# Second-phase transposes moved from TensorE to DMA, with five output buffers, paired score steps and a row-wise conv-state store

## The chip, the cores and the metric

One Trainium2 chip, all 8 NeuronCores, the same program on each core with its own data (one prompt sequence of 8192 tokens, and 16 of the 128 sample sequences with 8 tokens each). No core talks to another. The metric is the device time in microseconds (us) of the slowest core. The engines are TensorE (PE), VectorE (DVE), ScalarE (ACT), GpSimd (POOL) and SyncE (SP); SP and ACT issue DMAs on hardware queues (q1 and q10 in the profile), POOL on a software queue (q0).

## The reference

One layer of a hybrid decoder, cut to what matters:

```
xn = rmsnorm(x, g_attn);  q,k,v,B,C,h = split(xn @ w_in)          # 3072 columns
for g, (window, d) in enumerate([(128,1),(512,4),(2048,16)]):     # 4 heads of 64 per group
    s = q_g . k_g[t - d*(0..128)] / 8;  o_g = softmax(s) @ v_g;  lse_g = logsumexp(s)
attn = concat(o_g * softmax_over_groups(lse)_g)                    # 768 columns
u = C * h;  y = conv3(past ++ u);  conv = B * y                    # 256 columns
x1 = x + concat(attn, conv) @ w_out
x2 = x1 + relu(rmsnorm(x1, g_mlp) @ w_up)**2 @ w_down
out = rmsnorm(x2, g_fin)
```

It runs over the prompt (keys of the same sequence) and over the samples (keys from three caches of 128, 512 and 2048 rows, then the 8 new ones). Outputs besides `out`: the last rows of K and V of each group, and the last two rows of u (the conv state) for prompt and samples. For the samples the K/V outputs are the caches shifted by 8 rows, which the kernel copies DRAM to DRAM.

## The kernel before

All matmuls are bf16 with f32 accumulation. There are two phases with one order of work written out in Python; each engine walks the same list of steps and does its part, and semaphores tie them.

**First phase** (`make_plan`, `tensor_a`, `scalar_a`, `vector_a`, `sync_a`). Four super-tiles of 2048 tokens. For each: a block of 24 conv tiles (B, C, h projections), then for each of the three groups a block of 24 projection tiles (V, then Q and K). A tile is 8 or 16 matmuls into one of two PSUM banks and one evacuation by ACT or DVE; it is called a slot. While the tiles of one block run, the 16 attention chunks (128 queries) of the block before are spread between them: scores (step `S`: 8 matmuls, then one exponential on ACT), mask (`M`, DVE, one slot later), PV (PE, two slots later) and `O` (three slots later: DVE copies the 128 x 260 result from PSUM to one of two SBUF buffers `osb`, line 1029, and SP stores it to the DRAM tensor NZ, line 1316). The samples' projections come in one block after super-tile 0: their K and V rows go to `kvss` and from there to DRAM by 48 small stores on SP. The samples' conv state is loaded and stored by POOL with four DMAs each way (lines 1258 and 1253), 4 bytes at a time since channels lie on partitions: `in_=ubs[cc][:, :, 8 + j]` to `convs[:, j, ...].rearrange("b p -> p b")`. POOL also casts weights to bf16 DRAM to DRAM (`precast`, line 1248), computes the first tap of the convolution (line 1272), and at the end loads w_up and w_down.

**Second phase** (`tensor_b`, `scalar_b`, `vector_b`, `sync_b`). 33 tiles T, each of 256 tokens (the last, the samples', of 128) in subtiles of 128. The list `SLOTS` says what is done after each of the 36 slots c of tile T besides the MLP's own work, which is `up` c (8 matmuls, line 739) and `down` c-4 (4 matmuls, line 750): mostly the preparation of tile T+1.

- `LN`, `LX`, `LC`, `ST`: loads of NZ, x and conv output, store of y (SP)
- `a`: DVE normalises the attention sums into `attn_n` (which shares its memory with `xn1`)
- `b`: PE transposes `attn_n` (6 transposes, line 663), ACT copies PSUM to `attnT` (line 890)
- `c`: the output projection, two halves (line 678), DVE adds x (1126), ACT computes the norm (875 to 879)
- `n`: DVE scales to `xn1` (1133); `d`: PE transposes it (8 transposes, line 688), DVE multiplies by the gain into `xn1T` (1141)
- `sT`, `sS`, `sP`: one of 52 batches of the samples' cached attention: PE transposes the cached keys `sK` (8 transposes, line 701), DVE copies them (1091); scores; PV

Tile 0 is prepared in the last 16 slots of the first phase (`FIRST_B`), where only attention chunks are left. POOL starts w_up's load when the last projection is done and most of w_down's when the last NZ store has landed (lines 1278 to 1285). At slot 13 of every even tile ACT issues one sample's three cache copies (line 906; 4080, 1008 and 240 KB).

Of the kernel before, what the change touches and what calls it, by code (L numbers as in the profile page):

```python
# [44 lines left out]
class Waits:  # L45
# [6 lines left out]
    def wait_ge(self, sem, v):  # L52
        if v > self.got.get(sem.name, 0):
# [7 lines left out]
           (2, "b", 0, 0), (2, "LN", 1, 0), (3, "a", 0, 1), (4, "c", 0, 0, 0), (5, "b", 0, 1), (5, "LN", 1, 1),  # L61
           (6, "c", 0, 0, 1), (8, "c", 0, 1, 0), (9, "n", 0, 0), (10, "c", 0, 1, 1), (11, "d", 0, 0), (13, "n", 0, 1),
           (14, "d", 0, 1)]
# [48 lines left out]
def make_plan():  # L112
# [25 lines left out]
    def block(tiles, chunks, xs):  # L138
# [3 lines left out]
        for i, a in enumerate(chunks):  # L142
            at.setdefault(i * (ns - 1) // len(chunks), []).append(a)
        for i, tile in enumerate(tiles):
# [6 lines left out]
            if P.slot == 40:  # L151
                P.add("ldsc")
            if P.slot == 160:
                P.add("stcs")
# [37 lines left out]
    for st in range(4):  # L192
# [10 lines left out]
        for g in range(3):  # L203
# [41 lines left out]
            if st == 0 and g == 2:  # L245

                tiles = [(kind, None, dict(g=gg, t=t, p=p, copies=2 - t, xb=17)) for gg in range(3)
                         for kind, t, p in (("sq", 0, 0), ("sq", 0, 1), ("sq", 1, 0), ("sq", 1, 1))]
# [7 lines left out]
                          new("nS", 2, "act", 1), conv("C", 1), conv("H", 1), new("nP", 2, None, 2), new("nZ", 2, "dve", 2)]  # L256
# [3 lines left out]
                P.smp.update({(kw["kind"], kw["cc"]): kw for kind, kw in P.steps if kind == "proj" and kw["kind"] == "sconvH"})  # L260
# [29 lines left out]
def build_nc():  # L290
# [52 lines left out]
    ybuf = [mem.alloc("ybuf%d" % i, [128, 512], F32) for i in range(2)]  # L343
# [7 lines left out]
    osb = [mem.alloc("osb%d" % i, [128, 4, 65], F32) for i in range(2)]  # L351
# [7 lines left out]
    mem.off += 768  # L359
# [66 lines left out]
    B_M, B_T = 6, 7  # L426
# [14 lines left out]
    with ExitStack() as es:  # L441
# [15 lines left out]
        s_stnz = [sem("st_nz%d" % i) for i in range(2)]  # L457
# [7 lines left out]
        s_nm, s_stkvs, s_stcs = sem("n_masked"), sem("st_kvs"), sem("st_cs")  # L465
        s_ldk, s_ldv = sem("ld_cache_k"), [sem("ld_cache_v%d" % i) for i in range(2)]
        s_kt, s_ktc, s_ss, s_se, s_sm, s_sp, s_so = (sem("s_kt"), sem("s_kt_sb"), sem("s_scores"), sem("s_exp"),
                                                    sem("s_masked"), sem("s_pv"), sem("s_sum"))
# [297 lines left out]
        def copy_out(e, W, eng, a):  # L766
# [4 lines left out]
            if what in ("qk", "v", "kvt"):  # L771
# [4 lines left out]
                if a["kb"] == 2:  # L776
                    W.wait_ge(s_stkvs, 48 * 16)
# [681 lines left out]
```

## Time and profile before

| | |
|---|---|
| time, median of 3 runs | 3246.47 us (3242.42 to 3248.24) |
| time of the profiled execution | 3248.41 us |
| its span, slowest core (3) | 3246.7 us |
| spans of the 8 cores | 3194.0 to 3246.7 us, mean granted TensorE clock 0.979 to 0.987 |
| PE busy | 3035.3 us, 93% of the span |
| DVE, ACT, POOL busy | 41%, 33%, 6% |
| first phase, to the last projection of core 3 | about 1014 us |
| one second-phase tile with samples' batches | 66.7 us |
| one second-phase tile without them (from tile 27 on) | 65.2 us |

The profile is of one execution on the slowest core. "Idle before" tells for how long an engine had nothing to run before an instruction, and who released it. In the chain of waits the span is followed back from the last instruction, so only what stands there can shorten it. A DMA's "us to landing" runs from its issue to its last byte.

### The profile page before, as it was taken

How to read it: one execution, taken by the hardware profiler on the slowest of the kernel's cores; microseconds unless marked ns; L12 is line 12 of the kernel's file. 1: busy time of each engine (PE TensorE's matmuls, PEld its weight loads, DVE VectorE, ACT ScalarE, POOL GpSimd, SP SyncE). 2: the span in 40 equal slices, each digit the busy share in tenths (PEclk: the TensorE clock that was granted, in tenths of full speed). 3: DMA queues.
4: the chain of work that ended last, by engine and by line, in shares of the span. 5: the costliest groups of instructions: out<-in, count | busy, mean ns of one | idle time of the engine just before them, and what ended most of it. 6: DMA issues, size and time to landing. Idle time of an engine off the chain costs nothing.

```text
span 3246.7 us, 65561 instructions; the slowest of 8 cores (3194.0 to 3246.7 us)
## 1 busy us (share of the span) xinstructions
PE 3035.3 (93%) x23299; PEld 1948.8 (60%) x23299; DVE 1334.1 (41%) x2927; ACT 1080.6 (33%) x2399; POOL 187.3 (6%) x232
## 2 busy tenths in 40 slices
PE   5997859899997799999999999999999999999998
PEld 2654435565554466666666666666666666666665
DVE  5355426637444234333343333333343333433332
ACT  4244225436334223222232323323232233323232
POOL 3101200101000000000000000000000000000000
PEclk9998979999998899999999999999999999999999
DMA  9124925536134825444254343543535425333130
GB/s 198 37 67 115 79 43 130 129 70 149 34 131 178 206 51 132 104 103 120 55 141 109 86 119 58 155 109 69 122 64 145 121 57 125 77 117 107 38 114 21
DMA packets 168411, 331.62 MB, mean 102 GB/s; under 512 B 31840, under 2 KB 124000, under 8 KB 165984
## 3 DMA queue, kind: packets, MB, share of 16 engines
q1 hardware_dynamic: 94080, 172.92, 16.5%
q0 software_dynamic: 70672, 67.19, 15.9%
q10 hardware_dynamic: 3344, 87.30, 9.2%
q8 instruction: 198, 3.24, 0.5%
q14 instruction: 117, 0.96, 0.1%
HBM read 309.57 MB, written 176.39 MB: 150 GB/s over the span
## 4 chain that ended last, share of the span: by engine, by line
PE 84%; DMA 4%; ACT 3%; issue 3%; DVE 3%; SPq 1%; another core or an unknown queue 1%; POOL 0%; ACTq 0%; DVEq 0%; POOLq 0%
PE pp L750 28%; PE pp L739 26%; PE pp L566 12%; PE pp L678 7%; PE pp L533 4%; DMA NZ<-osb 3%; ACT junkB L875 1%; PE pp L536 1%; PE pp L688 1%; DMA w_in_sb<-w_in 1%; PE pp L582 1%; SPq L1328 1%; PE pp L701 1%; PE pp L663 1%; PE pp L511 1%
## 5 line engine op out<-in xcount | busy, mean ns | idle before, releaser
L739 PE MATMUL pp<-xn1T,w_up_sb 128*128 128x256 bf16 (+1 forms) x8448 | 1071.2, 271 | 29.3 <-ACT hr L901 26.6
L750 PE MATMUL pp<-w_down_sb,h1T 128*128 128x512 bf16 x4160 | 1057.9, 379 | 17.9 <-DMA w_down_sb<-w_down_b 17.9
L739 PEld LDWEIGHTS pp<-xn1T,w_up_sb 128*128 128x128 bf16 x8448 | 804.1, 98 | 281.1 <-issue 39.3
L901 ACT ACTIVATE hr<-pp 128x256 bf16<-128x256 f32 (+1 forms) x1056 | 394.6, 380 | 1181.6 <-PE pp L739 1173.9
L1150 DVE TENSOR_TENSOR h1T<-hr 128x256 bf16<-128x256 bf16 (+1 forms) x1056 | 301.0, 289 | 1003.1 <-ACT hr L901 936.5
L750 PEld LDWEIGHTS pp<-w_down_sb,h1T 128*128 128x128 bf16 x4160 | 402.7, 98 | 299.6 <-issue 19.0
L566 PE MATMUL pp<-xnT,w_in_sb 128*128 128x512 bf16 x2304 | 536.6, 382 | 24.2 <-DMA w_in_sb<-w_in 8.8
L566 PEld LDWEIGHTS pp<-xnT,w_in_sb 128*128 128x128 bf16 x2304 | 212.0, 98 | 268.9 <-issue 37.2
L678 PE MATMUL pp<-w_out_sb,attnT 128*128 128x512 bf16 x1040 | 249.7, 384 | 9.0 <-DMA attnT<-cvT 9.0
L858 ACT ACTIVATE PT<-pp 128x1024 bf16<-128x1024 f32 x171 | 174.2, 1023 | 145.3 <-PE pp L586 143.8
L1022 DVE TENSOR_TENSOR PT<-PT,mask 128x1024 bf16<-128x1024 bf16 (+1 forms) x192 | 129.4, 674 | 198.8 <-ACT PT L858 185.3
L875 ACT ACTIVATE junkB<-xtB 128x1024 bf16<-128x1024 f32 x130 | 137.1, 1055 | 195.4 <-DVE xtB L1126 192.0
L678 PEld LDWEIGHTS pp<-w_out_sb,attnT 128*128 128x128 bf16 x1040 | 102.3, 99 | 133.7 <-issue 13.9
L1126 DVE TENSOR_TENSOR xtB<-xtB,pp 128x512 f32<-128x512 f32 x130 | 89.5, 688 | 218.1 <-PE pp L678 218.0
L533 PE MATMUL pp<-w_in_sb,xnT 128*128 128x256 bf16 x1368 | 165.8, 278 | 8.6 <-issue 5.2
L533 PEld LDWEIGHTS pp<-w_in_sb,xnT 128*128 128x128 bf16 x1368 | 142.3, 118 | 23.0 <-issue 10.4
L1295 POOL DMA_DIRECT2D sK<-ck x52 | 38.7, 744 | 1668.4 <-PE pp L701 1668.4
L1158 DVE TENSOR_TENSOR xtB<-xtB,pp 128x512 f32<-128x512 f32 x130 | 80.7, 682 | 81.1 <-PE pp L750 81.1
L602 PE MATMUL pp<-V,PT 128*128 128x65 bf16 x624 | 60.4, 196 | 45.1 <-DVE PT L1022 26.4
L1029 DVE COPY osb<-pp 128x260 f32<-128x260 f32 x192 | 79.9, 421 | 48.5 <-DMA NZ<-osb 47.4
L1141 DVE TENSOR_TENSOR xn1T<-pp,g_mlp_sb 128x1024 bf16<-128x1024 bf16 x65 | 79.6, 1225 | 28.2 <-PE pp L688 28.0
L936 DVE TENSOR_TENSOR xnT<-pp,g_attn_sb 128x1024 bf16<-128x1024 bf16 x64 | 78.3, 1223 | 29.3 <-PE pp L511 28.7
(136 smaller groups left out, 1984.0 us busy)
## 6 DMA issues: line engine op xcount, KB each, us to landing
kvs<-ck ACTq DMA_DIRECT2D x16, 4080.0 KB, 21.2
xt<-xp SPq DMA_DIRECT2D x64, 512.0 KB, 5.3
xtB<-xp SPq DMA_DIRECT2D x64, 512.0 KB, 3.8
yp<-xtB SPq DMA_DIRECT2D x64, 512.0 KB, 3.1
NZ<-osb SPq DMA_DIRECT2D x192, 130.0 KB, 2.3
NZt<-NZ SPq DMA_DIRECT2D x64, 390.0 KB, 4.6
kvs<-ck ACTq DMA_DIRECT2D x16, 1008.0 KB, 6.4
sK<-ck POOLq DMA_DIRECT2D x52, 256.0 KB, 6.7
```

What stands on the lines that cost most here:

```text
L533: ins = e.matmul(b[:, i * 256:(i + 1) * 256], lhsT=toks, rhs=wi[:, kc, 512:768], start=kc == 0, stop=kc == 7)
L566: ins = e.matmul(b[:, 0:128] if smp else b, lhsT=wi[:, kc, col:col + 128], rhs=xr, start=kc == 0, stop=kc == 7)
L678: ins = e.matmul(bank(b_bank(T)[1]), lhsT=attnT[q % 2][:, kc, :], rhs=w_out_sb[:, kc, half[0] * 512:(half[0] + 1) * 512], start=kc == 0, s ...
L739: ins = e.matmul(bank(v % 2)[:, 0:N], lhsT=w_up_sb[:, i // 8, kc, (i % 8) * 128:(i % 8 + 1) * 128], rhs=xn1T[T % 2][:, kc, 0:N], start=kc ...
L750: ins = e.matmul(psD[s][:, half * 512:(half + 1) * 512], lhsT=h1T[v % NH][:, s * 128:(s + 1) * 128], rhs=w_down_sb[:, i, half * 512:(half ...
L858: e.activation(out=PT[k % NPT][:].rearrange("p b q x -> p (b q x)"), in_=ps.rearrange("p b x -> p (b x)"), func=AF.Exp, scale=0.125).then_ ...
L875: e.activation(out=junk, in_=src, func=AF.Square, accum_out=accs[0][r]).then_inc(s_bn, 1)
L901: e.activation(out=hr[v % NHR][:, 0:N], in_=bank(v % 2)[:, 0:N], func=AF.Relu).then_inc(s_hr, 1)
L1022: e.tensor_tensor(out=pt, in0=pt, in1=mask, op=ALU.mult).then_inc(s_mask, 1)
L1126: e.tensor_tensor(out=xh, in0=xh, in1=bank(b_bank(T)[1]), op=ALU.add).then_inc(s_x1, 1)
L1150: e.tensor_tensor(out=h1T[v % NH][:, 0:N], in0=hr[v % NHR][:, 0:N], in1=hr[v % NHR][:, 0:N], op=ALU.mult).then_inc(s_h1, 1)
L1158: e.tensor_tensor(out=xh, in0=xh, in1=psD[s][:, half * 512:(half + 1) * 512], op=ALU.add).then_inc(s_x2, 1)
```

## The change

Six edits:

1. **Transposes by DMA.** In the second phase the steps `b`, `t` (new, after `n`) and `sT` are DMA transposes issued by SP, SBUF to SBUF, 2-byte elements. PE's 44 transposes per tile and their PSUM copies go; `d` is now only the multiplication by the gain, in place in `xn1T`. The slots move: `b` right behind `a` (slots 5 and 9), `c` in slots 13 to 19 in place of 15 to 21, `t` in 20 and 24, `d` in 26 and 30, `sT` in 13 and 25.
2. **Five `osb` buffers** in place of two. For their room the conv buffer `ybuf` becomes the same memory as `Csb`.
3. **Samples' conv state by rows.** A new tile `su` computes C and h for the samples with tokens on partitions (8 matmuls of 512 columns), ACT and DVE form the product in `kvss`, and POOL stores two 1 KB rows per sample, 16 DMAs. The old store of four DMAs goes. The load (`ldsc`) is the same 4-byte pattern, cut in 16 pieces, one every second slot.
4. **Scores of two chunks behind one another**: chunks come in pairs in one slot, the second one's mask a slot later; both PV steps then stand behind one another.
5. POOL's loads of w_in for groups 1 and 2 come later (x tiles 13 and 16 in place of 7 and 12).
6. `FIRST_B` has the slots for tile 0's transposes.

```diff
 class Plan / make_plan
-            at.setdefault(i * (ns - 1) // len(chunks), []).append(a)
+            at.setdefault(i // 2 * 2 * (ns - 1) // len(chunks), []).append(a)
...
-            for a in at.get(i, ()):
+            for j, a in enumerate(at.get(i, ())):
                 P.add("S", **a)
-                P.later(1, "M", **a)
+                P.later(1 + j, "M", **a)
                 P.later(2, "PV", **a)
...
-    osb = [mem.alloc("osb%d" % i, [128, 4, 65], F32) for i in range(2)]
+    NO = 5
+    osb = [mem.alloc("osb%d" % i, [128, 4, 65], F32) for i in range(NO)]
...
 SLOTS (excerpt)
-                 7: [("y", -1, 1), ("ST", -1, 1), ("LX", 1, 1), ("b", 1, 0)], 9: [("a", 1, 1)], 11: [("b", 1, 1), ("LN", 2, 0)],
+                 7: [("y", -1, 1), ("ST", -1, 1), ("LX", 1, 1)], 9: [("a", 1, 1), ("b", 1, 1)], 11: [("LN", 2, 0)],
...
 tensor_b
-                    for kc in range(6):
-                        ins = e.transpose(out=pst[:, kc, :], in_=attn_n[:, kc * 128:(kc + 1) * 128], identity=ident[:])
-                    ins.then_inc(s_aT, 1)
...
 vector_a, step O
-                    if k >= 2:
-                        W.wait_ge(s_stnz[k % 2], 16 * (k // 2))
+                    if k >= NO:
+                        W.wait_ge(s_stnz[k % NO], 16 * (k // NO))
...
 pool
-                elif kind == "stcs":
-                    W.wait_ge(s_free["dve"], P.smp["sconvH", 1]["first"])
-                    for cc in range(2):
-                        for j in range(2):
-                            e.dma_start(out=convs[:, j, cc * 128:(cc + 1) * 128].rearrange("b p -> p b"),
-                                        in_=ubs[cc][:, :, 8 + j], allow_slow_non_contiguous=True).then_inc(s_stcs, 16)
+                elif kind == "proj" and a["kind"] == "su":
+                    W.wait_ge(s_free["dve"], a["first"])
+                    for bb in range(NSB):
+                        e.dma_start(out=convs[bb, :, :], in_=kvss[bb * 8 + 6:bb * 8 + 8, 256:512]).then_inc(s_stcs, 16)
...
 sync_b
+                elif kind == "b":
+                    q = nsubs_before(T) + i
+                    W.wait_ge(s_an, q + 1)
+                    if q >= 2:
+                        W.wait_ge(s_m, 2 * (q - 1))
+                    e.dma_start_transpose(out=attnT[q % 2][:, 0:6, :], in_=attn_n).then_inc(s_aT[q % 2], 16)
+                elif kind == "t":
...
+                    e.dma_start_transpose(out=xn1T[sl][:, :, i * 128:(i + 1) * 128], in_=xn1[:]).then_inc(s_xT1[q % 2], 16)
+                elif kind == "sT":
...
+                    e.dma_start_transpose(out=sKTc[:].rearrange("p u k t -> p (u k) t"),
+                                          in_=sK[:].rearrange("p u c -> p (u c)")).then_inc(s_kt, 16)
```

TensorE's order in the middle of a second-phase tile, before (L739 is `up`, L750 `down`, L678 the output projection `c`, L701 the transposes of cached keys, L663 those of `attn_n`):

```order
L739 MATMUL pp<-xn1T_9_120,w_up_sb_112 128x256 x8
L750 MATMUL pp<-w_down_sb_141,h1T_20_131 128x512 x4
L663 MATMUL pp<-ident_43,xn_8_119 128x128 x6
L739 MATMUL pp<-xn1T_9_120,w_up_sb_112 128x256 x8
L750 MATMUL pp<-w_down_sb_141,h1T_15_126 128x512 x4
L739 MATMUL pp<-xn1T_9_120,w_up_sb_112 128x256 x8
L750 MATMUL pp<-w_down_sb_141,h1T_16_127 128x512 x4
L739 MATMUL pp<-xn1T_9_120,w_up_sb_112 128x256 x8
L750 MATMUL pp<-w_down_sb_141,h1T_17_128 128x512 x4
L739 MATMUL pp<-xn1T_9_120,w_up_sb_112 128x256 x8
L750 MATMUL pp<-w_down_sb_141,h1T_18_129 128x512 x4
L678 MATMUL pp<-w_out_sb_111,attnT_6_117 128x512 x8
```

The same place after the change (there `up` is L714, `down` L725, `c` L675):

```order
L714 MATMUL pp<-xn1T_10_122,w_up_sb_113 128x256 x8
L725 MATMUL pp<-w_down_sb_142,h1T_19_131 128x512 x4
L714 MATMUL pp<-xn1T_10_122,w_up_sb_113 128x256 x8
L725 MATMUL pp<-w_down_sb_142,h1T_20_132 128x512 x4
L675 MATMUL pp<-w_out_sb_112,attnT_6_118 128x512 x8
L714 MATMUL pp<-xn1T_10_122,w_up_sb_113 128x256 x8
L725 MATMUL pp<-w_down_sb_142,h1T_15_127 128x512 x4
L714 MATMUL pp<-xn1T_10_122,w_up_sb_113 128x256 x8
L725 MATMUL pp<-w_down_sb_142,h1T_16_128 128x512 x4
L675 MATMUL pp<-w_out_sb_112,attnT_6_118 128x512 x8
```

The transposes between the MLP's matmuls are gone, and the output projection follows the fourteenth `up` of the tile in place of the sixteenth.

SP's order for one second-phase tile before, from the conv loads of the next tile on (L1377 `LC`, L1384 `ST`, L1371 `LX`, L1365 `LN`):

```order
L1377 DMA attnT_6_117<-cvT 128x2x128
L1377 DMA attnT_7_118<-cvT 128x2x128
L1384 DMA yp<-xtB_3_114 128x1024
L1371 DMA xtB_3_114<-xp 128x1024
L1384 DMA yp<-xtB_3_114 128x1024
L1371 DMA xtB_3_114<-xp 128x1024
L1365 DMA NZt_4_115<-NZ 128x780
L1365 DMA NZt_5_116<-NZ 128x780
```

And after (L1350 `LC`, L1376 `ST`, L1344 `LX`, L1338 `LN`, L1358 `b`, L1364 `t`, L1370 `sT`):

```order
L1376 DMA yp<-xtB_3_115 128x1024
L1344 DMA xtB_3_115<-xp 128x1024
L1358 DMA_TRANSPOSE attnT_6_118<-xn_8_120 128x6x128
L1376 DMA yp<-xtB_3_115 128x1024
L1344 DMA xtB_3_115<-xp 128x1024
L1358 DMA_TRANSPOSE attnT_7_119<-xn_8_120 128x6x128
L1338 DMA NZt_4_116<-NZ 128x780
L1338 DMA NZt_5_117<-NZ 128x780
L1370 DMA_TRANSPOSE sKTc_139<-sK_136 128x8x128
L1364 DMA_TRANSPOSE xn1T_10_122<-xn_8_120 128x8x128 x2
L1370 DMA_TRANSPOSE sKTc_139<-sK_136 128x8x128
L1350 DMA attnT_6_118<-cvT 128x2x128
```

Six transposes are now in SP's queue; each of the two `b` stands directly behind a load of x.

In the first phase TensorE ran one chunk's scores and PV between two projection tiles (L582 and L586 are scores, L602 and L603 PV, L566 a projection tile):

```order
L582 MATMUL pp<-Q_33_76,K_35_78 128x128 x2
L586 MATMUL pp<-Q_33_76,K_35_78 128x128 x2
L582 MATMUL pp<-Q_33_76,K_35_78 128x128 x2
L586 MATMUL pp<-Q_33_76,K_35_78 128x128 x2
L566 MATMUL pp<-xnT_52,w_in_sb_8_51 128x512 x8
L582 MATMUL pp<-Q_33_76,K_35_78 128x128 x2
L586 MATMUL pp<-Q_33_76,K_35_78 128x128 x2
L582 MATMUL pp<-Q_33_76,K_35_78 128x128 x2
L586 MATMUL pp<-Q_33_76,K_35_78 128x128 x2
L566 MATMUL pp<-xnT_52,w_in_sb_8_51 128x512 x8
L602 MATMUL pp<-V_37_80,PT_38_81 128x65
L603 MATMUL pp<-V_37_80,PT_38_81 128x65
```

After the change (L583, L587 scores, L603, L604 PV, L567 projection) two chunks' scores stand together, and so do two chunks' PV:

```order
L567 MATMUL pp<-xnT_52,w_in_sb_8_51 128x512 x8
L583 MATMUL pp<-Q_31_74,K_33_76 128x128 x2
L587 MATMUL pp<-Q_31_74,K_33_76 128x128 x2
L583 MATMUL pp<-Q_31_74,K_33_76 128x128 x2
L587 MATMUL pp<-Q_31_74,K_33_76 128x128 x2
L583 MATMUL pp<-Q_31_74,K_33_76 128x128 x2
L587 MATMUL pp<-Q_31_74,K_33_76 128x128 x2
L583 MATMUL pp<-Q_31_74,K_33_76 128x128 x2
L587 MATMUL pp<-Q_31_74,K_33_76 128x128 x2
L567 MATMUL pp<-xnT_52,w_in_sb_8_51 128x512 x16
L603 MATMUL pp<-V_35_78,PT_37_80 128x65
```

Fewer changes between scores and projection tiles are left, and two tiles in a row have none beside them.

## Rows read from the trace of the kernel before

**Rows 1.** Span and granted clock of core 7.

```profile
core 7: 3245.1 us, clock 0.981
```

**Rows 2.** Core 3: length; PE, PEld, DVE, ACT, POOL busy; clock; DMA share; GB/s.

```profile
399.84:498.50 98.66, 59.63 (x514) 36.22 (x513) 23.90 (x43) 23.20 (x28) 1.95 (x4) 0.78 0.38 48
665.04:717.60 52.56, 52.56 (x515) 33.75 (x513) 23.82 (x43) 23.20 (x28) 1.95 (x4) 1.00 0.36 77
1485.78:1552.50 66.72, 65.97 (x496) 43.92 (x494) 25.14 (x64) 20.17 (x52) 2.96 (x4) 1.00 0.57 145
```

**Rows 3.** Costliest groups: the transposes (count; busy us, mean ns; idle before).

```profile
L688 PE MATMUL pp<-ident,xn 128*128 128x128 bf16 x520 | 40.0, 220 | 0.3 <-DVE xn L1133 0.3
...
L663 PE MATMUL pp<-ident,xn 128*128 128x128 bf16 x384 | 32.5, 222 | 0.0
...
L701 PE MATMUL pp<-ident,sK 128*128 128x128 bf16 x416 | 31.7, 219 | 0.0
```

**Rows 4.** Timeline of PE in one tile: start us, us, instructions.

```profile
1497.36 0.50 PE L663 MATMUL pp<-ident,xn 128*128 128x128 bf16 x6
1497.69 1.04 PE L739 MATMUL pp<-xn1T,w_up_sb 128*128 128x256 bf16 x8
...
1499.43 1.04 PE L739 MATMUL pp<-xn1T,w_up_sb 128*128 128x256 bf16 x8
```

**Rows 5.** Timelines of SP and of DVE in one tile.

```profile
1498.06 0.35 SPq L1371 DMA_DIRECT2D xtB<-xp  x1
...
1501.38 0.16 DVE L1077 TENSOR_TENSOR stats<-NZt 128x4 f32<-128x4 f32 x1
...
1519.09 11.22 SPq L1377 DMA_DIRECT2D attnT<-cvT  x2
...
1528.19 0.75 DVE L1133 TENSOR_SCALAR xn<-xtB,stats 128x1024 bf16<-128x1024 f32 x1
...
1538.78 0.74 DVE L1133 TENSOR_SCALAR xn<-xtB,stats 128x1024 bf16<-128x1024 f32 x1
```

**Rows 6.** DMA issues: queue, count, KB each, median us to landing.

```profile
kvs<-ck ACTq DMA_DIRECT2D x16, 4080.0 KB, 21.2
...
xtB<-xp SPq DMA_DIRECT2D x64, 512.0 KB, 3.8
...
NZ<-osb SPq DMA_DIRECT2D x192, 130.0 KB, 2.3
...
convs<-ubs POOLq DMA_DIRECT2D x4, 8.0 KB, 51.6
```

**Rows 7.** The same for DMAs issued from 1513 to 1520 us.

```profile
attnT<-cvT SPq DMA_DIRECT2D x1, 64.0 KB, 12.4
```

**Rows 8.** Chain of waits, core 3: start us, us, what.

```profile
417.59 41.94 DMA NZ<-osb
...
951.61 13.95 DMA NZ<-osb
...
1020.40 16.85 DMA NZ<-osb
...
1067.13 13.98 DMA w_down_sb<-w_down_b
...
1102.56 17.25 another core or an unknown queue
```

**Rows 9.** Timeline of POOL: the conv-state store's issue.

```profile
371.06 4.65 POOL L1253 DMA_DIRECT2D convs<-ubs  x4 [0.25 <-issue]
```

**Rows 10.** Chain of waits, core 7.

```profile
410.91 13.77 issue
...
437.00 19.04 DMA NZ<-osb
```

**Rows 11.** Chain of waits, core 3, around scores and PV.

```profile
465.90 1.83 PE pp L566 x8
...
467.98 1.73 PE pp L566 x8
```

More of the change, by code:

```diff
@@ L342, in build_nc @@
     Csb = [mem.alloc("Csb%d" % i, [128, 512], F32) for i in range(2)]
-    ybuf = [mem.alloc("ybuf%d" % i, [128, 512], F32) for i in range(2)]
+    ybuf = Csb
     cvo = [mem.alloc("cvo%d" % i, [128, 512], BF16) for i in range(2)]
@@ L456, in build_nc @@
         s_hk, s_hv = sem("halo_k"), sem("halo_v")
-        s_stnz = [sem("st_nz%d" % i) for i in range(2)]
+        s_stnz = [sem("st_nz%d" % i) for i in range(NO)]
         s_cvch, s_cv, s_cvtail, s_tap = sem("conv_chain"), sem("conv_out"), sem("conv_tail"), sem("conv_tap")
@@ L519, in tensor_a @@
                     W.wait_ge(s_xnT, a["xb"])
[L520 to L521 removed]
+                    wi = w_in_sb[0] if what[-1] in "BCHu" else w_in_sb[1 + a["g"]]
+                    if what[-1] in "BCHu":
                         W.wait_ge(s_ldw[0], 16)
@@ L882, in scalar_b @@
             for kind, T, i, *half in events:
[L883 removed]
                 n = NORM.get((kind, T, i))
[L885 to L891 removed]
+                if kind == "c" and half[0] == 1:
                     q = nsubs_before(T) + i
@@ L959, in vector_a @@
                         continue
+                    if what == "su":
+                        W.wait_ge(s_proj, a["full"])
+                        W.wait_ge(s_uc, 1)
+                        e.tensor_tensor(out=kvss[:, 256:512], in0=bank(n % 2)[:, 256:512], in1=kvss[:, 0:256],
+                                        op=ALU.mult).then_inc(s_free["dve"], 1)
+                        continue
                     if what[-1] != "H":
@@ L1039, in vector_a, with stored @@
                                   ).then_inc(s_hk, 1)
+        def stored(W, n):
+            for i in range(NO):
+                W.wait_ge(s_stnz[i], 16 * ((n + NO - 1 - i) // NO))
         def phase_a_left(W):
@@ L1236, in pool @@
             for kind, a in STEPS:
-                if kind == "xc" and a["k"] in (7, 12):
-                    load_w_in(1 if a["k"] == 7 else 2)
+                if kind == "xc" and a["k"] in (13, 16):
+                    load_w_in(1 if a["k"] == 13 else 2)
                 elif kind == "xc" and a["k"] == 8:
@@ L1282, in pool @@
                     W.wait_ge(s_pv, 192)
-                    for i in range(2):
-                        W.wait_ge(s_stnz[i], 16 * 96)
+                    stored(W, 192)
                 e.dma_start(out=w_down_sb[:, lo:hi, :], in_=w_down_v[:, lo:hi, :]).then_inc(s_wd[k], 16)
@@ L1352, in sync_b @@
                     W.wait_ge(s_xT, 65)
-                    for k in range(2):
-                        W.wait_ge(s_stnz[k], 16 * 80)
+                    stored(W, 160)
                 elif kind in ("LN", "LC"):
                     phase_a_left(W)
-                    for k in range(2):
-                        W.wait_ge(s_stnz[k], 16 * (88 if T < 2 else 96))
+                    stored(W, 176 if T < 2 else 192)
                 if kind == "up" and T == 0 and i == 0:
```

147 lines of the change are left out of this document (56 added, 91 removed), and 10 rows, old and new, of tables (FIRST_B, SLOTS).

## The prediction

> **What bounds the kernel now.** I read the stretches first. A second-phase tile takes 66.7 us and PE is busy for 66.0 of them, at the full granted clock; DVE has 25 us of work in it, ACT 20 (third of [rows 2]). That phase is some 2130 of the 3247 us, so there the time is PE's own work and what leaves PE leaves the span, as long as nothing else comes late. The costliest groups then give what could leave: 520, 384 and 416 transposes [rows 3]. In the first phase two equal blocks of 24 projection tiles and 16 chunks take 98.7 and 52.6 us (first two of [rows 2]): the same 59.6 against 52.6 us of PE work, but 39 us of idle PE and a mean clock of 0.78 in the first. The chain of waits names the idle time: 41.9 us of NZ<-osb from 417.6 on, then 14.0 and 16.9 us at the end of the phase, and 14.0 and 17.3 us behind w_down [rows 8].
>
> **Transposes off PE.** Six transposes occupy PE from 1497.36 to 1497.69, until the next `up` begins: 0.33 us, 55 ns each [rows 4] (the mean of 220 ns in [rows 3] is latency in a pipeline). Tile 0's two subtiles lie in the transition and don't count. What counts is (384/6 - 2) x 0.33 = 20.5 us, (520/8 - 2) x 8 x 0.055 = 27.7 us and 416 x 0.055 = 22.9 us: 71 us. DVE loses its copy of the keys and ACT its copy of attnT, which were hidden.
>
> What must hide the new transfers: a slot is 1.74 us (1497.69 to 1499.43) [rows 4]. Where the trace has no SBUF-to-SBUF transpose, I bound its landing by the nearest rows: 2.3 us (130 KB NZ store) and 3.8 us (512 KB load) below, 12.4 us above, for 64 KB issued on SP's queue while the 4080 KB cache copy was in flight [rows 6, 7]. A transpose moves 192 or 256 KB, so I take 4 us from issue, plus the rest of what stands ahead of it on the queue.
>
> - `b` of subtile 0 is issued behind the x load of 1498.06. DVE starts `a` of subtile 1 at 1501.38 [rows 5] and now waits there for the transpose, since `attn_n` is one buffer: 3.0 us after the issue at 1498.4. Behind the waiting instruction stand the h1T squares, which `down` needs four slots after `up`: 7 us, less the 2 us of ACT and DVE in between. So landing within 3 + 5 = 8 us costs nothing. The x load ahead lands at 1498.06 + 3.8 = 1501.9; with 4 us more it is 1505.9, that is 7.5 us after the issue. Hidden, but by half a microsecond: this is the tightest place, 32 times.
> - `t` of subtile 0 follows `n`. The two `n` write at 1528.19 and 1538.78 [rows 5], four slots and one half of `c` apart as in the new order; less the 0.75 us write and 0.44 us of transposes that is 9.4 us for the landing, plus DVE's 5. In every even tile the cache copies run: they are issued at slot 13, near 1485.8 + 13 x 1.74 = 1508.4, and the largest lands 21.2 us later [rows 6], about 1530; `t` is issued at 1528.2 - 2 slots - 1.1 us of transposes + 0.75 = 1524.4, and even if it lands only 4 us behind the copies that is 1534, where the second `n` would start (1533.8). Hidden.
> - `t` of subtile 1 has six slots, 10.4 us. `sT` is issued at the time the copies start and scored 10 slots later, 24 us with the four halves of `c`: hidden too.
> - SP issues six more DMAs per tile and stands still for each condition. Behind `sT` (waits for the key load) are `t` and the next tile's stores; the key load was landed long before in the trace. The row at 1519.09 shows SP waiting 11.2 us inside a pair of loads without anybody waiting for it [rows 5].
>
> So nothing is taken off the 71 us; the ends are 71 and, with 12.4 us for each `b`, 71 - 32 x 4.4 = -70 us.
>
> **Conv state by rows.** POOL issues the store at 371.06 [rows 9]; its landing takes 51.6 us for 8 KB [rows 6], and until 460 the NZ stores are stuck. The block that this hits costs 98.66 - 52.56 = 46.1 us too much [rows 2]. On core 7 the same place shows 13.8 + 19.0 = 32.8 us [rows 10]. 16 DMAs of 2 KB in 1 KB rows are no such load: -46 on core 3, -33 on core 7 (ends 0 and -50). Against it: one tile of 8 matmuls of 512 columns, 1.7 us like the projection tile in [rows 11], and 16 DMAs on POOL at 1.2 us for each instruction at most (4.65/4) [rows 9], up to 19 us in which the next block's first tap is late. The tap's wait reaches PE only through the next copy of the same channels, six tiles (10 us) later, which hides most: +3 (0 to +12). The load cut in 16 pieces lies in a block where it moved nothing before: 0.
>
> **Pairs of chunks.** A projection tile behind scores takes 1.83 us, behind PV 1.73 [rows 11]. 88 pairs save one such change each: 9 us. ACT gets two exponentials in a row, but its work in such a block is 23.2 of 52.6 us (second of [rows 2]), and it stays the same: fits. In the three conv blocks DVE is the fuller engine and bursts could cost what pairs give: -9 (ends -18 and +10).
>
> **Five buffers.** With three more buffers PE and DVE run three chunks on (6 us) before a late store stops them. Of the 14.0 us at 951.6 [rows 8] I take off 8. At the phase's end the stores share the queues with w_up's load; of 16.9 us and the smaller waits behind it perhaps 20 go, w_down's load starts as much earlier since it waits for the last store, but the 31 us behind w_down (14.0 + 17.3) remain, and tile 0's four transposes now go through busy DMA queues, 12.4 us each in place of about 2 on PE and ACT. Net -10 (ends -35 and +25). The later w_in loads: 0.
>
> **The sum** on core 3's execution of 3248.4 us: -71 - 46 + 3 - 9 - 8 - 10 = -141, 3107. On core 7, 3245.1 [rows 1] + 1.7 us around the span - 71 - 33 + 3 - 9 - 8 - 10 = 3119. The slowest core decides, and part of what core 7 lost was at a low clock: 3113. The runs shown have their median 1.9 us under the profiled one: **3111 us**.
>
> **A rule that speaks against it.** The Trainium skill, "VectorE: DVE Perf Modes", section "The three transpose paths", gives 390 ns for a 128x128 bf16 transpose on TensorE and 1309 ns through DMA. This trace has 55 ns of PE time for the first, since such transposes overlap; the second no run shows yet. As an estimate from that page, eight in series would be 10.5 us and six 7.9 us, and `b` would land at 1501.9 + 7.9 = 1509.8, 11.4 us after its issue: 3.4 us late in each of 32 tiles, 109 us. "DMA: Bandwidth & Descriptors", "Latency and other measured facts", has 261 GB/s for transposes, by which 256 KB would be about 1 us plus the fixed cost, as an estimate.
>
> **Rivals.**
> 1. *The transposes land a little late.* Between 8 and 12.4 us after issue: every microsecond over 8 is 32 us in all. For it: the half microsecond of margin at `b`. Against: the 2.3 and 3.8 us of plain DMAs. Middle 10.2 us: 3111 + 70 = 3181 us.
> 2. *The stall at 400 us stays.* POOL's weight casts are in the same software queue, and they rather than the 4-byte store could hold up NZ. For it: the casts stand in that queue too. Against: 8 KB that needs 51.6 us. 3111 + 46 = 3157 us.
> 3. *Slower: a serial transpose.* If a DMA transpose takes more than 12.4 us, its price per tile at `b` is its landing less 8, from 14.4 us on also at the first `t` and soon at the second, each on the way to the next tile's first `up`. At 16 us: 8.0 + 1.6 + 0.7 = 10.3 us x 32 = 330 us, 3441 us. It is slower than before from a loss of 4.2 us per tile, a landing of 12.2 us. For it: small elements are what the store of 4-byte pieces suffers from (8 KB in 51.6 us), and a transpose has 2-byte elements. Against: nothing else in the trace.
>
> **Chances.** Forecast 0.64, rival 1 0.14, rival 2 0.09, rival 3 0.13. The forecast's own range is 3075 to 3150. The range of 8 in 10 goes from 3070 (the good ends of pairs and buffers, 9 + 25 us less, and some us for core 7's clock) to 3225, which takes in rival 2 and most of rival 1 and leaves rival 3 out. 0.2% (6 us) is about what a measurement can tell; between the cases almost nothing lies there: faster 0.86, same 0.02, slower 0.12.
>
> **What would show it.** Second-phase tiles of 64.2 us with samples' batches (66.7 - 4 x 0.44 - 2 x 0.33 = 64.3); transposes landing in 4 to 8 us; no wait of DVE on attn_n that reaches PE; no idle PE around 400 to 460 us; the two block lengths equal at some 52 us. Wrong if: DVE's `a` waits over 5 us for the transpose and PE's `up` or `down` waits for h1T or xn1T, or the last chunks' waits grow because tile 0's transposes stand behind the weight loads.

## The result and the profile after

The changed kernel takes 3520.2 us (median of four executions; 3479.8 to 3586.5) against 3246.6 us of before: 1.080 times as long, 95% interval 1.071 to 1.090. The forecast was 3111 us. Executions in which the cores of one die ran at a lower granted clock (here one, without which the median is 3511.1 us) are left out of every ratio and of every time from here on. The runs below were made on three chips, on which the kernel before took 3243 to 3248 us, so a difference of a few us between two of them means nothing.

The page is that of core 6, the slowest of the profiled execution (3511.1 us). Its chain is 67% PE and 13% DMA. Two of its DMA queues, SP's and ACT's (packets, MB, share of 16 engines):

```profile
q1 hardware_dynamic: 268832, 216.20, 31.5%
...
q10 hardware_dynamic: 3344, 87.30, 10.3%
```

Where PE waited (engine, line, releaser: us in total, times, longest):

```profile
PE pp L689 <- DMA sKTc<-sK: 141.5, 9, 37.5
PE pp L675 <- DMA attnT<-xn: 134.7, 7, 40.3
PE pp L603 <- DVE PT L1000: 50.3, 31, 8.5
PE pp L714 <- issue: 38.4, 2, 25.2
```

The first and second are the sample scores and the output projection, both waiting for a transpose: 276 us in only 16 waits. So the typical transpose is not slow; a few are very slow. Core 6 is not special in this: on the other seven the two waits come to 115 to 261 us. The DMA issues say the same. First the view of the issues (count, KB, median landing) with the counterparts of [rows 6], then the three transposes by tile (issue time min/median/max in ns; landing min/median/max in us).

```profile
kvs<-ck ACTq DMA_DIRECT2D x16, 4080.0 KB, 39.0
...
xtB<-xp SPq DMA_DIRECT2D x64, 512.0 KB, 4.2
...
xn1T<-xn SPq DMA_TRANSPOSE x65, 3.5
attnT<-xn SPq DMA_TRANSPOSE x64, 4.5
sKTc<-sK SPq DMA_TRANSPOSE x52, 5.4
```

```profile
L1364 SPq DMA_TRANSPOSE xn1T<-xn x65: 1231/1233/37023, 1053.2 to 3447.6; - x65
DMA to landing us min/median/max: 3.0/3.5/52.4
```

```profile
L1370 SPq DMA_TRANSPOSE sKTc<-sK x52: 1231/1258/50505, 1159.8 to 3089.5; - x52
DMA to landing us min/median/max: 2.7/5.4/68.4
```

The median landings are what I forecast (4 us from issue). The maxima are not: on every core the worst transpose of the keys lands after 62 to 78 us. The cache copy beside them, 21.2 us in [rows 6], now has a median of 39.0, and 24.3 to 32.2 on the other cores.

A place where it happens, in an even tile. ACT issues the copies at 1892.96 and SP the transpose of the keys at 1893.36, as the new plan has both at up number 13. The timeline of SP (start, us):

```profile
1893.36 1.23 SPq L1370 DMA_TRANSPOSE sKTc<-sK  x1
1910.18 54.95 SPq L1364 DMA_TRANSPOSE xn1T<-xn  x2
```

And stretches of 10 us (length; PE, PEld, DVE, ACT, POOL busy; clock; DMA share; GB/s):

```profile
1900.00:1910.00 10.00, 9.89 (x62) 6.10 (x63) 3.14 (x7) 3.01 (x8) 0.00 (x0) 1.00 0.91 113
1910.00:1920.00 10.00, 4.78 (x32) 2.99 (x31) 1.31 (x4) 2.25 (x6) 0.00 (x0) 0.85 0.95 162
1920.00:1930.00 10.00, 0.00 (x0) 0.00 (x0) 0.00 (x0) 0.00 (x0) 0.00 (x0) 0.50 1.24 48
1930.00:1940.00 10.00, 0.01 (x1) 0.01 (x1) 0.00 (x0) 0.00 (x0) 0.00 (x0) 0.50 1.08 71
```

Read the last two columns together: the DMA engines are full (share over 1) and move 48 to 71 GB/s, where a tile of before with the same copies moved 145 at a share of 0.57 [rows 2]. Everything else stands still, and the granted clock of PE falls to the lower of its clock levels (0.50 of 2.4 GHz). SP is held 37 us inside one issue, and 54.95 us pass over two of them. The keys' transpose, issued at 1893.36, lands after 68.4 us.

Whose packets fill the engines there, from 1920 to 1960 us (packets, MB, share of 16 engines)?

```profile
q1 hardware_dynamic: 874, 0.22, 106.2%
q10 hardware_dynamic: 44, 1.76, 15.4%
```

It is SP's queue, with the transposes, and not the copy's. Its packets take 1.062 x 16 x 40 us / 874 = 0.78 us each. In 16 us of a run without the copies (the first experiment below), with three transposes and two small loads, from 1508 to 1524 us, they took 0.352 x 16 x 16 / 3712 = 0.024 us each:

```profile
q1 hardware_dynamic: 3712, 0.92, 35.2%
```

The longest stop of PE in this stretch is not a wait for a transposed tile. PE breaks off inside a group of eight matmuls and goes on 25 us later, with "issue" as the reason, that is, with nothing that the profile can name:

```profile
1914.29 0.49 PE L714 MATMUL pp<-xn1T,w_up_sb 128*128 128x256 bf16 x3
1939.99 1.23 PE L714 MATMUL pp<-xn1T,w_up_sb 128*128 128x256 bf16 x5 [25.21 <-issue]
```

In that gap the queue that the page calls "instruction", q8, moves one packet of 16 KB, which starts at 1937.7, 2.3 us before PE goes on. The eight cores have 13 such stops of over 5 us in the second phase (5.3 to 37.0 us); in each one a packet of q8 starts 2.3 to 2.6 us before its end. In the second phase of before, and of the runs below without copies or with the copies in the gap, there is no such stop. So it seems that PE's next instructions come by DMA as well and were stuck at the full engines. That is read from the times alone and not shown; no run moves the fetch by itself.

In the first phase two lengths answer to [rows 2]. The block that had the stall is whole; the stretch with the conv tiles behind it is not (the same columns).

```profile
403.96:455.25 51.29, 50.64 (x508) 33.55 (x513) 23.80 (x43) 22.67 (x29) 1.94 (x4) 1.00 0.37 79
455.25:596.14 140.89, 117.47 (x1074) 69.55 (x1088) 90.78 (x145) 72.32 (x125) 15.04 (x15) 0.95 0.50 127
690.07:831.52 141.45, 117.29 (x1074) 69.69 (x1088) 90.75 (x145) 72.33 (x125) 14.10 (x13) 0.95 0.41 105
```

Before, the same conv stretches of core 3 took

```profile
498.34:622.19 123.85, 114.29 (x1094) 67.45 (x1091) 91.31 (x146) 73.72 (x126) 16.56 (x15) 1.00 0.57 145
717.44:841.25 123.81, 114.45 (x1095) 67.40 (x1092) 91.95 (x147) 73.72 (x126) 15.44 (x13) 1.00 0.48 119
```

So there are three suspects: transposes beside the cache copies (276 us of waits for them, and 38 of the other kind), the conv stretches (17 us each), and the transition, where the chain of waits shows

```profile
1012.05 23.92 DMA attnT<-xn
...
1081.34 19.20 DMA attnT<-xn
1102.49 37.83 DMA attnT<-xn
```

The first of these belongs to tile 0. The third begins after ACT has issued the first sample's copies at 1096.8, so it is a case of the first suspect too.

### The profile page after: what moved, and what is told of

The parts are those of the page before. It is cut to its first block, busy times and chain, and to the rows that moved or that the text cites. A ratio compares the mean times of both kernels' runs of the same rounds, so it can differ in the third digit from the quotient of the medians.

```text
span 3509.5 us, 62403 instructions; the slowest of 8 cores (3325.3 to 3509.5 us)
## 1 busy us (share of the span) xinstructions
PE 2960.5 (84%) x21625; PEld 1882.5 (54%) x21987; DVE 1297.9 (37%) x2876; ACT 1017.8 (29%) x2336; POOL 195.2 (6%) x256
## 3 DMA queue, kind: packets, MB, share of 16 engines
q1 hardware_dynamic: 268832, 216.20, 31.5%
q10 hardware_dynamic: 3344, 87.30, 10.3%
## 4 chain that ended last, share of the span: by engine, by line
PE 67%; DMA 13%; issue 5%; DVE 5%; another core or an unknown queue 4%; ACT 3%; SPq 1%; POOL 1%; DVEq 0%; ACTq 0%; POOLq 0%
PE pp L725 22%; PE pp L714 21%; PE pp L567 11%; DMA attnT<-xn 6%; PE pp L675 5%; DMA sKTc<-sK 5%; PE pp L534 3%; DMA yp<-xtB 1%; ACT junkB L854 1%; DVE PT L1000 1%; PE pp L537 1%; DMA w_in_sb<-w_in 1%; POOL Csb L1248 1%; DVE Csb L967 1%
## 5 line engine op out<-in xcount | busy, mean ns | idle before, releaser
L714 PE MATMUL pp<-xn1T,w_up_sb 128*128 128x256 bf16 (+1 forms) x8448 | 1082.9, 273 | 66.3 <-issue 38.4
L725 PE MATMUL pp<-w_down_sb,h1T 128*128 128x512 bf16 x3930 | 1022.2, 381 | 14.7 <-DMA w_down_sb<-w_down_b 2.5
L714 PEld LDWEIGHTS pp<-xn1T,w_up_sb 128*128 128x128 bf16 x8448 | 815.8, 98 | 348.7 <-issue 74.6
L725 PEld LDWEIGHTS pp<-w_down_sb,h1T 128*128 128x128 bf16 x4160 | 406.2, 98 | 307.9 <-issue 22.5
L567 PE MATMUL pp<-xnT,w_in_sb 128*128 128x512 bf16 x2219 | 522.9, 387 | 24.0 <-DMA w_in_sb<-w_in 9.1
L675 PE MATMUL pp<-w_out_sb,attnT 128*128 128x512 bf16 x1007 | 255.1, 392 | 137.2 <-DMA attnT<-xn 134.7
L567 PEld LDWEIGHTS pp<-xnT,w_in_sb 128*128 128x128 bf16 x2304 | 218.6, 99 | 270.9 <-issue 41.3
L675 PEld LDWEIGHTS pp<-w_out_sb,attnT 128*128 128x128 bf16 x1040 | 103.3, 100 | 265.4 <-issue 150.7
L837 ACT ACTIVATE PT<-pp 128x1024 bf16<-128x1024 f32 x171 | 166.2, 1024 | 136.7 <-PE pp L587 136.4
L534 PE MATMUL pp<-w_in_sb,xnT 128*128 128x256 bf16 x1368 | 158.0, 273 | 3.7 <-DVE V L739 3.7
L689 PE MATMUL pp<-sQz,sKTc 128*128 128x2 bf16 (+2 forms) x416 | 18.2, 165 | 141.5 <-DMA sKTc<-sK 141.5
L603 PE MATMUL pp<-V,PT 128*128 128x65 bf16 x624 | 55.3, 195 | 87.0 <-DVE PT L1000 50.3
L689 PEld LDWEIGHTS pp<-sQz,sKTc 128*128 128x128 bf16 x416 | 17.8, 97 | 156.2 <-issue 146.0
L603 PEld LDWEIGHTS pp<-V,PT 128*128 128x128 bf16 x624 | 45.4, 98 | 98.5 <-issue 92.2
```

The lines of the kernel that those rows point to most:

```text
L534: ins = e.matmul(b[:, i * 256:(i + 1) * 256], lhsT=toks, rhs=wi[:, kc, 512:768], start=kc == 0, stop=kc == 7)
L567: ins = e.matmul(b[:, 0:128] if smp else b, lhsT=wi[:, kc, col:col + 128], rhs=xr, start=kc == 0, stop=kc == 7)
L603: e.matmul(po[:, h, :], lhsT=PT[k % NPT][:, hh, p, 0:128], rhs=vprev(h), start=True, stop=False)
L675: ins = e.matmul(bank(b_bank(T)), lhsT=attnT[q % 2][:, kc, :], rhs=w_out_sb[:, kc, half[0] * 512:(half[0] + 1) * 512], start=kc == 0, stop ...
L714: ins = e.matmul(bank(v % 2)[:, 0:N], lhsT=w_up_sb[:, i // 8, kc, (i % 8) * 128:(i % 8 + 1) * 128], rhs=xn1T[T % 2][:, kc, 0:N], start=kc ...
L725: ins = e.matmul(psD[s][:, half * 512:(half + 1) * 512], lhsT=h1T[v % NH][:, s * 128:(s + 1) * 128], rhs=w_down_sb[:, i, half * 512:(half ...
```

## The experiments

Theory A: a transpose and a cache copy that are in flight together hold each other up. Theory B: the transposes, or SP's queue, are late by themselves. Theory C: the first phase's edits are the loss. The edits have the numbers of the section on the change: 1 transposes, 2 buffers, 3 conv state, 4 pairs, 5 w_in loads.

**No cache copies.** Leaves out the copied part of the samples' cache outputs.

```diff
-                        for g in range(3):
+                        for g in ():
                             e.dma_start(out=kvs[g][b, 0:WIN[g] - 8, :], ...)
```

> The changed kernel without the 48 cache copies of the second phase (their part of the outputs is left out); all else as changed. Theory A (a transpose by DMA and a cache copy that are in flight at the same time hold each other up): the landings over 20 us go, tiles take 64 to 66 us, and the time falls by about 350 us to 3090-3170 us. Theory B (the transposes come late by themselves, or because SP's instructions stand behind one another): the waits for attnT, xn1T and sKTc stay, over 3400 us. Theory C (the loss lies in the other edits, in the first phase): the copies aren't there, so the loss stays, over 3300 us with second-phase tiles that are already at 64 us in both.

Measured: 0.9776 of before (0.9718 to 0.9835, from two executions), its profiled execution 3174.1 us. None of PE's larger waits is for a transpose, and the keys' worst landing is 8.5 us:

```profile
DMA to landing us min/median/max: 2.8/4.8/8.5
```

Nearly 340 us (3511.1 less 3172.2) come back with the copies gone. B and C have no room left for the main loss. It doesn't yet tell the copies' traffic from their moment.

**Transposes on PE, all other edits.** The diff without edit 1: the planner's and the buffers' lines changed, `b`, `d` and `sT` on PE as before.

> The kernel before with edits 2 to 5 (conv state by rows, pairs of chunks, five output buffers, later w_in loads); transposes on PE as before. Theory A: no stall in the second phase, and the first phase gains what the forecast gave it less what pairs cost: 3185 to 3240 us. Theory B: the same. Theory C: 3300 us or more.

Measured: 1.0002 of before (0.9969 to 1.0036), 3236.5 us in the profiled execution. C falls as the main cause. But the first phase gives nothing, where I had forecast 57 us on core 7 and 70 on core 3: something in it takes back what the vanished stall gives.

**Transposes by DMA alone.**

> The kernel before with the transposes by DMA alone (edit 1). Theory A and B: as slow as the changed kernel or worse, 3500 to 3620 us. Theory C: faster than before by the 71 us of the forecast, about 3175 us.

Measured: 1.1012 of before (1.081 to 1.122, from two executions), 3599.8 us in the profiled one. PE waits 364.8 us for the keys on its slowest core, and 156 to 280 us on the others:

```profile
PE pp L687 <- DMA sKTc<-sK: 364.8, 13, 56.2
```

Edit 1 is the whole loss, and it is the step I had counted as -71 us.

**Copies in the gap.** Each sample's copies in halves, in two tiles, where no transpose should be in flight.

```diff
-                    if T % 2 == 0 and T < 32 and i == 13:
+                    if T < 32 and i == 29:
                         b = T // 2
                         for g in range(3):
-                            e.dma_start(out=kvs[g][b, 0:WIN[g] - 8, :], in_=ck[g][b, 8:WIN[g], :])...
+                            n = (WIN[g] - 8) // 2
+                            lo = n * (T % 2)
+                            e.dma_start(out=kvs[g][b, lo:lo + n, :], in_=ck[g][b, 8 + lo:8 + lo + n, :])...
```

> The changed kernel; each sample's copies are cut in halves and issued in two following tiles at up number 29 in place of 13, where the last transpose of the tile should have landed and the next is issued some 12 slots (20 us) later. The same bytes are moved in the same phase. Theory A: nearly no landing over 20 us for a transpose in the tiles, 3120 to 3200 us. Theory B: as the changed kernel, 3450 us or more. A rival within A (it is the load on the memory as a whole, over the entire phase, and not what is in flight together): little changes, 3400 us or more.

Measured: 3170.1 us (3169.0 to 3171.1 in four executions), 0.977 of before (0.974 to 0.980). The same bytes in the same phase, 341 us less. The tile has the length that the forecast gave, 64.3 us (columns as in [rows 2]):

```profile
1143.08:1207.36 64.28, 63.56 (x453) 41.53 (x451) 24.65 (x64) 18.63 (x50) 2.97 (x4) 1.00 0.57 131
```

The share of the DMA engines is 0.57, the same as in [rows 2]; it is not the load of the tile but what stands beside what. The halves land in 11.1 us in the median, the worst `xn1T` in 6.0, the worst keys in 8.5. Theory B is gone: the same transposes on the same queue are on time once the copies stand elsewhere.

**The same without pairs**, **pairs alone**, and **rows and buffers without pairs**, for the first phase.

```diff
-            at.setdefault(i // 2 * 2 * (ns - 1) // len(chunks), []).append(a)
+            at.setdefault(i * (ns - 1) // len(chunks), []).append(a)
```

> The changed kernel with the copies in halves at up number 29 and without edit 4 (chunks one by one again, spread evenly). Theory P (pairs cost about 40 us, in the three conv blocks, since two chunks' masks and copies reach DVE in a burst that PV waits for): 3125 to 3140 us. Rival Q (pairs are free, and what the conv blocks lost comes from the other first-phase edits: shared buffer of the conv, no longer stalled elsewhere): within 10 us of 3170, or 3180 with the forecast's 9 us given back.

> The kernel before with edit 4 alone (pairs of chunks). Theory P: 25 to 45 us slower than before, 3270 to 3290 us. Rival Q: within 10 us of before.

> The kernel before with edits 2, 3 and 5 (conv state by rows, five output buffers sharing the conv's buffer, later w_in loads), no pairs, transposes on PE. Theory P: 3190 to 3210 us, the 33 to 46 us of the stall at 400 us off the time before. Rival Q: near 3240 us, as with pairs.

Measured: without pairs 3135.3 us (3132.9 to 3137.3), 34.8 less than with them, both with the copies in the gap. Pairs alone are slower than before by 0.8% (1.0081, 1.0042 to 1.0121; 26 us). Rows and buffers alone give 1.0% (0.9902, 0.9864 to 0.9939; 32 us). Theory P holds in all three, and -32 and +26 to 35 are why the second experiment showed nothing. Edits 2, 3 and 5 were not run apart from each other. The place of the pairs' cost is the conv stretches: with them PE waits there for the masks (in the first of the two stretches above),

```profile
PE pp L603 <- DVE PT L1000: 18.7, 11, 2.9
```

and without them not at all, the stretch being back at 123.5 us with DVE as busy as before (91.7 us of it); the plain block costs 52.55 against 51.29:

```profile
401.79:454.34 52.55, 52.55 (x513) 33.76 (x512) 23.70 (x42) 23.19 (x28) 1.95 (x4) 1.00 0.35 77
454.34:577.81 123.47, 114.30 (x1094) 67.52 (x1091) 91.73 (x146) 73.68 (x126) 15.86 (x15) 1.00 0.59 145
```

**Small packets at the old moment.** Copies of the changed kernel as even and odd rows, so that no piece is over 2 KB.

```diff
-                            e.dma_start(out=kvs[g][b, 0:WIN[g] - 8, :], in_=ck[g][b, 8:WIN[g], :])...
+                            dst = kvs[g][b, 0:WIN[g] - 8, :].rearrange("(n t) c -> t n c", t=2)
+                            src = ck[g][b, 8:WIN[g], :].rearrange("(n t) c -> t n c", t=2)
+                            for t in range(2):
+                                e.dma_start(out=dst[t], in_=src[t])...
```

> The changed kernel, copies issued at up number 13 as there, but each as two DMAs of even and odd rows, so that no piece is longer than 2 KB (before up to 64 KB). The same bytes. Theory A1 (a transpose's small packets wait behind the long packets of the copy, engine by engine): the stalls shrink to a fraction, under 3300 us. Theory A2 (any DMA traffic of this size beside the transposes does it, the length of its packets being no matter): 3400 us or more.

Measured: 1.0264 of before (1.022 to 1.031), 3331.7 us; between what A1 and A2 expected. PE hardly waits for a transpose any more (7 us on this core) but for ACT, whose issues of the copies take up to 11.0 us (the last of a sample's six, in most samples), and whose first instruction behind them is late:

```profile
ACT hr L873 <- issue: 157.6, 18, 15.6
```

The worst landing of the keys falls from 68.4 to 29.7 us. This is a hint for packet length, mixed with a cost of the experiment itself; hence the pair of runs with pieces below.

**Copies whole, but later.** One number of the changed kernel: `i == 13` becomes `i == 29`.

> The changed kernel with one number changed: each sample's copies, whole as there, are issued at up number 29 of every even tile in place of 13. The largest took 21.2 us by itself before, so it should be done at about up 5 of the next tile, when the next transpose is issued. Theory A: 3165 to 3220 us (as the halves, 3170 us, plus some copies that reach into the next tile's first transposes). Rival (cutting in halves is what helped, not the moment): 3400 us or more.

Measured: 1.0399 of before (1.032 to 1.048, from two executions), 3383.9 us in the profiled one: outside what A expected, since I had put the copy at 21 us beside transposes, and just under the 3400 us of the rival. Its cores tell why:

```profile
core 1: 3382.4 us, clock 0.954
core 2: 3153.0 us, clock 0.985
```

On core 1 the copy's median landing is 33.9 us, which reaches into `b` of the next tile:

```profile
PE pp L675 <- DMA attnT<-xn: 172.8, 16, 12.8
```

16 waits for 16 samples. On core 2 it lands in 19.5 us, before that point, and PE has no such wait:

```profile
kvs<-ck ACTq DMA_DIRECT2D x16, 4080.0 KB, 19.5
```

Same program, same execution; the core whose copies are done before the transposes is 230 us shorter. All eight cores fall in this order: where the copy lands in 19.5, 22.4, 25.4, 27.7, 28.5, 30.8, 32.5 and 33.9 us, the span is 3153, 3183, 3301, 3306, 3322, 3329, 3378 and 3382. That bears out A, and speaks for halves helping because they end in time. Why the same copy takes 20 us on one core and 34 on another isn't shown. No such wait is over 12.8 us on core 1, where the changed kernel had 40.3: what the number of transposes beside a copy does wasn't tried either.

**Pieces, long and short.** Both cut a sample's copies into 15 parts at up numbers 13 to 22; the second makes two DMAs of each, of even and odd rows.

```diff
-                    if T % 2 == 0 and T < 32 and i == 13:
+                    if T % 2 == 0 and T < 32 and 13 <= i < 23:
                         b = T // 2
-                        for g in range(3):
+                        for g, np in ((0, 1), (1, 4), (2, 10)):
+                            n = (WIN[g] - 8) // np
+                            lo = n * (i - 13)
+                            if i - 13 < np:
+                                e.dma_start(out=kvs[g][b, lo:lo + n, :], in_=ck[g][b, 8 + lo:8 + lo + n, :])...
```

> The changed kernel; the copies of a sample are cut in 15 DMAs (10, 4 and 1 of a group), issued one to three an up from number 13 to 22, each with packets as long as it allows (up to some 26 KB). The control of the next kernel. Theory A1 (a transpose's 256-byte packets wait behind long packets): stalls remain, over 3350 us. Theory A2 (it is the mere presence of other traffic): over 3350 us as well.

> As the kernel with 15 DMAs a sample, at the same up numbers, but each as two DMAs of even and odd rows: no packet over 2 KB, about 100 a DMA, so that ACT is not held up for 11 us at an issue as it was with 1020. Theory A1: the stalls are gone and ACT's too, 3170 to 3220 us. Theory A2: as its control.

Measured: long 1.0357 (1.028 to 1.044), 3356.4 us in the profiled execution; short 1.0289 (1.023 to 1.035), 3338.2 us. The times hardly differ, which would speak for A2; the landings do, and they are what A1 is about. `xn1T` long, then short:

```profile
DMA to landing us min/median/max: 3.0/4.1/33.9
```

```profile
DMA to landing us min/median/max: 3.0/4.8/11.8
```

The keys: at most 44.3 us against 12.2. It holds on every core: the worst `xn1T` lands after 26.7 to 41.8 us with long pieces and 10.8 to 12.2 with short ones, the worst keys after 32.3 to 51.1 and 10.4 to 13.8. What the short pieces save there, ACT pays: 30 issues a sample at 0.79 us in the median, in place of 15 at 0.52, and `hr` waits behind them:

```profile
ACT hr L873 <- issue: 204.9, 67, 6.5
```

PE feels it: its waits for transposes fall from 150.6 us to 8.0, and those for `hr` rise from 26.4 us to

```profile
PE pp L714 <- ACT hr L873: 150.4, 121, 5.0
```

So the length of the packets beside it makes the worst landings, shown at equal up numbers and bytes (the number of DMAs differs, 15 against 30, and the short ones are issued more slowly); my expected 3170 to 3220 us was wrong because I left the issuing engine's time out.

**Tile 0 on PE.** The kernel without pairs, copies in the gap, and the four transposes of tile 0 as before the change.

```diff
+                if kind in ("b", "d") and T == 0:
+                    pst = bank_bf(0).rearrange("p (k t) -> p k t", k=8)
...
+                    for kc in range(6 if kind == "b" else 8):
+                        ins = e.transpose(out=pst[:, kc, :], in_=..., identity=ident[:])
...
+                elif kind in ("b", "t") and T == 0:   # SP
+                    pass
```

> The kernel of 3135 us (copies in the gap, no pairs) with the transposes of tile 0 on PE as before, those of all other tiles by DMA. Before them the chain showed 24.0 us of attnT and 3.1 us of xn1T. If these were what the transition lost (my step on the five buffers, 12.4 us each): 3110 to 3120 us. If w_down's load would have held tile 0 up anyway: 3128 to 3138 us.

Measured: 3115.6 us (3114.9 to 3116.5), 0.9585 of before (0.953 to 0.964), 19.7 us under the kernel with them by DMA, or 26 by the two ratios. The wait of 24.0 us for tile 0's attnT, which the chain of that kernel has, is gone, and two for NZ, 10.0 and 13.5 us, stand in its place; tile 1's, still by DMA and still beside w_down's load, stay in the chain:

```profile
1027.82 17.16 DMA attnT<-xn
1046.93 11.00 DMA attnT<-xn
```

This is the fastest version; those without copies or with the copies in the gap also beat both kernels.

## Why the prediction was wrong

The step that failed is the one on what must hide the transposes, in every even tile, where the cache copies run. From the changed kernel down to the fastest version the runs take three steps: 3511.1 - 3170.1 = 341 us for the copies' moment, 34.8 for the pairs and 19.7 for tile 0, together 396. That the last kernel ends at 3115.6 us, so near the forecast of 3111, is in part luck: it has neither the pairs, for which the forecast took off 9 us, nor tile 0's transposes, for which it put on 42. By the forecast's own terms it would be 3111 + 9 - 42 = 3078. The 38 us over that go to the forecast for edits 2, 3 and 5 in the main, which was too good.

*Transposes off PE (-71).* The saving itself is real: with the copies moved, tiles take 64.28 us against the forecast's 64.3, and the kernel with edits 2, 3 and 5 goes from 3208.5 us (median) to 3135.3, which is 73 us less. The step at `b` with its half microsecond of margin held, with landings of 4.5 us in the median: DVE waited 3.9 us there each time (126.2 us in 32), and no wait of PE for h1T came of it on core 6. What failed is the sentence on `t` of subtile 0, "even if it lands only 4 us behind the copies that is 1534 ... Hidden", and with it that on `sT`, "hidden too". I took the copy's 21.2 us of [rows 6] as a constant and let only the transpose be late. In flight together both are late: 39.0 us in the median (24 to 32 on other cores) and up to 67.5 for the copy, up to 52.4 and 68.4 for the transposes. In place of -71 the step cost 328 us by itself (1.1012 of before). The cover was 24 us for the keys and 9.4 + 5 for `t`. The row that warned was on the list: a 64 KB load took 12.4 us against a median of 2.8 with this copy in flight [rows 7]. I used it as the upper end for a transpose at `b`, where no copy was due, and not at `t` and `sT`, where one was. A transpose is some (268,832 - 94,080) / 181 = 965 packets, all under 512 B, against 256 of that load.

The mechanism, as far as it is shown: the loss is there only with copy and transpose in flight together, and shorter packets in the copy cut the worst landing from 33.9 to 11.8 us at the same moment. How the packets hold each other up isn't settled. The Trainium skill, "DMA: Bandwidth & Descriptors", section "Queues, rings and completion order", says that an engine goes round the queues that have work and changes only at a packet's end (a packet there holds several descriptors, so it need not be what the profile counts as one). That agrees in direction with these landings: the copies' queue has 87.3 MB in 3344 packets, 26 KB each on average, against some 250 B. But it isn't the whole of it: from 1920 to 1960 us the long packets fill only 15% of the engines, and the transposes' own packets take 0.78 us each in place of 0.024. The same skill's "Advanced Engine Details and Errata", "X-Bar Transpose (TRN2)", calls transposes as fast as regular DMAs; in the median they are, 3.5 us for `xn1T` against 4.2 for the x load, and beside the copies not.

*Rivals.* Rival 3 had the sign and nearly the price (10 us a tile, 3441 us) but another mechanism, a transpose that is slow every time. Rival 1's waits of a few microseconds at `b` didn't come. Rival 2 is refuted: the stall is gone (98.66 to 51.29 us) while the casts are still issued in that block, and ten of them from 360 to 470 us now land in 5.6 us in the median, where five took 41.8 before. The kernels that keep the 4-byte store (transposes alone, pairs alone) keep the stall; the new store lands in 1.7 us where 51.6 stood in [rows 6].

*Conv state, buffers (-46 or -33, +3, -18).* For edits 2, 3 and 5 my sum on core 7 is -48, on core 3 -61, and both still carry the cost of tile 0's transposes, which the run without edit 1 doesn't have; measured -32 with an interval of -20 to -44. Core by core, the odd ones got 33 to 38 us shorter and the even ones, which were some 30 us shorter to begin with, 4 to 22. The stall is gone as forecast, so what is too large is in the rest: the buffers' -18, or the 16 issues on POOL, for which I had +3 and of which the chain shows 7.9 us near 297. The -10 in it doesn't follow from the parts that I named beside it: 20 us off, w_down's load as much earlier, 42 on. Not taken apart further.

*Pairs (-9).* Wrong in sign: +26 to +35 us, outside the ends of -18 and +10. In the plain blocks the saving came (52.55 to 51.29 us, 1.3 each, eight blocks: some 10 us). But "bursts could cost what pairs give" was sized by nothing. In a conv stretch DVE is busy 91 of 124 us; two masks behind one another there make PV wait 11 times, and 17 to 18 us a stretch are lost, more in one than my upper end of +10 for all.

*Transition.* I had tile 0's landings at 12.4 us each; the first attnT took 24.0. Size only: its removal gave 20 to 26 us, against the 50 - 8 = 42 us that four at 12.4 would have cost if nothing else held the tile up; something else does, as the two waits for NZ show.

## What to carry to other kernels

Before moving work to a DMA, list what else is in flight at each of its moments, and bound both by what happens when they overlap, not by either one's landing alone; the largest transfer with the longest packets is the one to look at. A landing's maximum says more than its median: all three transposes had a median under 5.5 us here, and cost some 340. Where a background transfer can be put anywhere, cut it so that it ends inside a stretch without short, urgent DMAs; and count the issuing engine's time for every extra piece. A schedule that evens out the fuller engine's work shouldn't be bunched to save a switch of another.

## What the runs showed of the hardware

- With transposes and a long-packet copy between DRAM tensors in flight, the DMA engines are full and move 48 to 71 GB/s, against 131 in an undisturbed tile at a share of 0.57. The transposes' packets then take 0.78 us each in place of 0.024, and the copy, too, lands after 39.0 us in place of 21.2. Why the packets get so slow isn't settled.
- SP is held in the issue of a transpose, normally 1.2 us, for up to 50.5 us. Core 6 has nine such holds of over 15 us; in eight of them an earlier transpose was still under way. What stands behind it on the queue is late as well.
- In the same stretches PE stops with no tile to wait for, for 5 to 37 us, and goes on 2.3 to 2.6 us after a packet of the instruction queue q8 starts, 13 times out of 13 on the eight cores. A full set of DMA engines seems to keep instructions from PE as well as data; this is read from times and was not tried apart.
- The issue of a DMA of 1020 rows of 2 KB took ACT 0.84 us; that of a second one right behind it, the last of a sample's six, took 2 to 11.0 us in 13 of 16 samples. One of 102 such rows took 0.79 us in the median, up to 3.8 in the series of 30.
